# GpSimd takes the border sums of the second network, the border's roots follow directly, and a stage splits its first weight unit alone

## The reference

```python
for layer in range(DEPTH):
    u = rms_norm_2(h, norm_g[layer, 0]) * (1.0 + sc1) + sh1
    y = hgrn2_mixer(...) if layer % N_MIXERS == 0 else dilated_attention_mixer(...)
    h = h + (1.0 + g1) * rms_norm_2(y, norm_g[layer, 1])
    u = rms_norm_2(h, norm_g[layer, 2]) * (1.0 + sc2) + sh2
    y = swiglu_ffn(u, ffn_w_in[layer], ffn_w_out[layer])
    h = h + (1.0 + g2) * rms_norm_2(y, norm_g[layer, 3])
```

## Time and profile before

| | us |
|---|---|
| median of 3 runs (lowest to highest) | 3851.92 (3847.77 to 3854.98) |
| the profiled execution | 3851.2 |
| its span, first to last instruction | 3849.4 |
| PE busy | 3546.0 (92%) |
| DVE busy | 1979.5 (51%) |
| ACT busy | 1365.0 (35%) |
| POOL busy | 4.6 (0%) |

### The profile page before, as it was taken

One profiled execution on the slowest core, in us unless ns is written; L12 is line 12 of the kernel. 1 busy time (PEld: TensorE's weight loads), 2 busy tenths in 40 slices (PEclk: granted clock), 3 DMA queues, 4 the chain that ended last, 5 costly groups with the idle time before them and its releaser, 6 DMA issues.

```text
span 3849.4 us, 43254 instructions
## 1 busy us (share of the span) xinstructions
PE 3546.0 (92%) x18038; PEld 2888.2 (75%) x18038; DVE 1979.5 (51%) x2741; ACT 1365.0 (35%) x1914; POOL 4.6 (0%) x13
## 2 busy tenths in 40 slices
PE   7899988999999999789997997999879999969997
PEld 3685547888888755588886776888778888768886
DVE  5436446777445454465545556433455545563335
ACT  3322343422323333353345445422443333362223
POOL 0000000000000000000000000000000000000000
PEclk9999998999999999999998998999989999989998
DMA  4331013445443230145532221222222323212221
GB/s 173 131 117 54 11 33 107 135 153 164 132 142 119 79 104 0 44 149 176 183 110 66 55 66 55 88 90 96 77 73 66 93 68 88 65 55 98 89 96 47
DMA packets 366626, 360.68 MB, mean 94 GB/s; under 512 B 65072, under 2 KB 312031, under 8 KB 365024
## 3 DMA queue, kind: packets, MB, share of 16 engines
q1 hardware_dynamic: 366211, 357.84, 30.1%
q10 hardware_dynamic: 220, 0.07, 0.0%
HBM read 350.02 MB, written 4.72 MB: 92 GB/s over the span
## 4 chain that ended last, share of the span: by engine, by line
PE 44%; DVE 6%; ACT 6%; issue 2%; DMA 0%; SPq 0%; DVEq 0%; ACTq 0%
PE ps L402 38%; ACT second_w_hi L472 1%; PE ps L2503 1%; DVE second_w_lo L530 1%; DVE r_st L2397 1%; DVE sums L463 1%; PE ps L2524 1%; ACT second_scr L668 1%; PE ps L2526 1%; PE ps L2276 1%; PE ps L2513 1%; DVE second_scr L852 0%; DVE x_res L854 0%; DVE second_scr L679 0%; DVE sq L460 0%
## 5 line engine op out<-in xcount | busy, mean ns | idle before, releaser
L402 PE MATMUL ps<-second_h_hi,second_w_hi 128*128 128x512 f32 (+1 forms) x2216 | 833.4, 376 | 117.4 <-DVE second_h_lo L880 59.0
L402 PE MATMUL ps<-second_h_lo,second_w_hi 128*128 128x512 f32 (+1 forms) x2216 | 813.8, 367 | 0.0
L402 PE MATMUL ps<-second_h_hi,second_w_lo 128*128 128x512 f32 (+1 forms) x2216 | 813.3, 367 | 0.0
L530 DVE TENSOR_TENSOR second_w_lo<-ring,second_w_hi 128x2048 fp32r<-128x2048 f32 (+2 forms) x176 | 373.2, 2121 | 505.6 <-ACT second_w_hi L472 505.6
L402 PEld LDWEIGHTS ps<-second_h_hi,second_w_hi 128*128 128x128 f32 x2216 | 432.9, 195 | 185.2 <-issue 72.6
L402 PEld LDWEIGHTS ps<-second_h_lo,second_w_hi 128*128 128x128 f32 x2216 | 432.9, 195 | 63.6 <-issue 1.7
L402 PEld LDWEIGHTS ps<-second_h_hi,second_w_lo 128*128 128x128 f32 x2216 | 431.0, 194 | 65.4
L472 ACT ACTIVATE second_w_hi<-ring 128x2048 fp32r<-128x2048 f32 (+2 forms) x176 | 311.4, 1770 | 348.7 <-PE ps L402 337.1
L402 PE MATMUL ps<-h_mix_hi,w_hi 128*128 128x512 f32 (+3 forms) x776 | 276.7, 357 | 27.8 <-DVE h_mix_lo L695 17.7
L402 PE MATMUL ps<-h_mix_lo,w_hi 128*128 128x512 f32 (+3 forms) x776 | 273.1, 352 | 0.0
L402 PE MATMUL ps<-h_mix_hi,w_lo 128*128 128x512 f32 (+3 forms) x776 | 272.5, 351 | 0.0
(11 more groups left out here) (402 smaller groups left out, 5726.6 us busy)
## 6 DMA issues: line engine op xcount, KB each, us to landing
ring<-in_w_mlp SPq DMA_DIRECT2D x64, 1024.0 KB, 5.3
side_w<-in_ada_w SPq DMA_DIRECT2D x96, 512.0 KB, 4.3
ring<-in_ffn_w_in SPq DMA_DIRECT2D x44, 1024.0 KB, 5.1
side_w<-in_w_mod SPq DMA_DIRECT2D x80, 512.0 KB, 3.8
ring<-in_attn_w_in SPq DMA_DIRECT2D x48, 512.0 KB, 5.2
ring<-in_hgrn_w_in SPq DMA_DIRECT2D x32, 512.0 KB, 4.8
ring<-in_ffn_w_out SPq DMA_DIRECT2D x16, 1024.0 KB, 4.9
ring<-in_w_in SPq DMA_DIRECT2D x14, 1024.0 KB, 5.4
```

The lines of the kernel that those rows point to most:

```text
L402: mm = pe.matmul(acc, lhsT, rhs, start=k == 0 and wp == ap, stop=k == j.kt - 1 and wp == 1)
L530: dve.tensor_tensor(unit.place(unit.slot[1]), unit.place(M.ring[:, u % RING, :]), unit.place(unit.slot[0]), ALU.subtract).then_inc(*S.w_lo ...
```

## The change

Five edits. (1) `add_sums` runs on GpSimd in a queue of its own instead of on DVE; `sums_now` and `pending` go. (2) For the sums of the last border (`sums_last`, gain 7) the square with the gain and the product are left out and only one part of three is added, since only the first root is used there. (3) `BorderThread`: ACT takes the second root directly behind the first, without the yield between; DVE's steps begin at(1) instead of at(2), and so each one job earlier; ACT's scale and high parts come at(2) and at(3) instead of both at(3). (4) At the start of a stage unit 0 alone is split, then the threads at -1 run, then the other units. (5) Behind a summed job of the second half (`slow`), DVE splits a freed unit's low part one job later. The new flag `by_pool` is set nowhere, so the first network's squares stay where they are.

```diff
     def square_sums(self, act, j):
...
         act.activation(dst[:, 0, :], y, ACT.Square)
-        act.activation(dst[:, 2, :], y, ACT.Square, scale=g)
+        if not j.sums_last:
+            act.activation(dst[:, 2, :], y, ACT.Square, scale=g)
         act.activation(y, y, ACT.Identity, scale=g, bias=0.0).then_inc(*S["sums_act"].one)
-    def add_sums(self, dve, j):
+    def add_sums(self, pool, j):
...
         if fresh:
-            dve.tensor_tensor(acc[:, 1, :], y, x, ALU.mult).then_inc(*S["sums_added"].one)
+            pool.tensor_tensor(acc[:, 1, :], y, x, ALU.mult).then_inc(*S["sums_added"].one)
             return
         dst = self.scratch(j)
-        dve.tensor_tensor(dst[:, 1, :], y, x, ALU.mult).then_inc(*S["sums_dve"].one)
-        dve.wait_ge(S["sums_dve"].sem, S["sums_dve"].at(S["sums_dve"].sent))
-        dve.wait_ge(S["sums_added"].sem, S["sums_added"].at(j.sum_nth))
-        dve.tensor_tensor(acc, acc, dst, ALU.add).then_inc(*S["sums_added"].one)
+        parts = slice(0, 1 if j.sums_last else 3)
+        if not j.sums_last:
+            pool.tensor_tensor(dst[:, 1, :], y, x, ALU.mult).then_inc(*S["sums_product"].one)
+            pool.wait_ge(S["sums_product"].sem, S["sums_product"].at(S["sums_product"].sent))
+        pool.wait_ge(S["sums_added"].sem, S["sums_added"].at(j.sum_nth))
+        pool.tensor_tensor(acc[:, parts, :], acc[:, parts, :], dst[:, parts, :], ALU.add).then_inc(*S["sums_added"].one)
+
+    def gpsimd(self, pool):
+        S, M = self.S, self.M
+        for j in self.jobs:
...
+            if j.sums:
+                self.add_sums(pool, j)
+        yield 0
     def scalar(self, act):
-        u = 0
+        u = 1
+        self.high(act, 0)
+        yield -1
         while u < len(self.units) and self.freed(u) < 0:
             self.high(act, u)
             u += 1
-        yield -1
     def vector(self, dve):
-        u, pending = 0, None
+        u = 1
+        self.low(dve, 0)
+        yield -1
         while u < len(self.units) and self.freed(u) < 0:
             self.low(dve, u)
             u += 1
-        yield -1
...
-            if pending:
-                self.add_sums(dve, pending)
-            pending = None
-            if j.sums and j.sums_now:
-                self.add_sums(dve, j)
-            elif j.sums:
-                pending = j
-            while u < len(self.units) and self.freed(u) <= j.at:
+            while u < len(self.units) and self.freed(u) <= j.at - j.slow:
                 self.low(dve, u)
                 u += 1
 class NormThread(Thread):
-    def high_parts(self, act, step):
+    def high_parts(self, act, step, pace=0.5):
         for i in range(self.n_batches):
-            yield self.at(step + i // 2)
+            yield self.at(step + int(i * pace))
 class BorderThread(NormThread):
     def scalar(self, act):
...
         act.preload_act_table_set("natural_log")
-        yield self.at(2)
         act.wait_ge(S["post_mean"].sem, S["post_mean"].at(n + 1))
...
-        yield from self.high_parts(act, 3)
+        yield from self.high_parts(act, 2, 1)
     def vector(self, dve):
-        yield self.at(2)
+        yield self.at(1)
...
-        yield self.at(3)
+        yield self.at(2)
         self.residual(dve, 1)
         self.product(dve, 1)
         for i in range(self.n_batches):
-            yield self.at(4 + i)
+            yield self.at(3 + i)
     def summed(js, gain):
-            j.sums_now = b == KD - 1
+            j.sums_last, j.slow = gain == 7, a > 0
```

More of the change, by code:

```diff
@@ L250, in __init__ @@
         self.needs, self.after, self.weights_first = needs, after, weights_first
-        self.square, self.wide, self.sums = square, None, None
+        self.square, self.wide, self.sums, self.by_pool, self.slow = square, None, None, False, False
 def cut(w, r0, r1, c0, n=UNIT, jobs=()):
@@ L453, in add_sums @@
         for sig, n in j.sums_after:
-            dve.wait_ge(sig.sem, sig.at(n))
-        dve.wait_ge(S["sums_act"].sem, S["sums_act"].at(j.sum_nth + 1))
+            pool.wait_ge(sig.sem, sig.at(n))
+        pool.wait_ge(S["sums_act"].sem, S["sums_act"].at(j.sum_nth + 1))
         if fresh:
-            dve.tensor_tensor(acc[:, 1, :], y, x, ALU.mult).then_inc(*S["sums_added"].one)
+            pool.tensor_tensor(acc[:, 1, :], y, x, ALU.mult).then_inc(*S["sums_added"].one)
             return
         dst = self.scratch(j)
-        dve.tensor_tensor(dst[:, 1, :], y, x, ALU.mult).then_inc(*S["sums_dve"].one)
-        dve.wait_ge(S["sums_dve"].sem, S["sums_dve"].at(S["sums_dve"].sent))
-        dve.wait_ge(S["sums_added"].sem, S["sums_added"].at(j.sum_nth))
-        dve.tensor_tensor(acc, acc, dst, ALU.add).then_inc(*S["sums_added"].one)
+        parts = slice(0, 1 if j.sums_last else 3)
[7 more added lines that the diff above has]
+        for j in self.jobs:
+            if j.by_pool:
+                n = j.n
+                for done, added, nth, dst, i in ((S.sq_act, S.sq_add, j.square_nth, j.square[1], 0),
+                                                 (S["wide_act"], S["wide_add"], j.wide_nth, j.wide[1], 1)):
+                    pool.wait_ge(done.sem, done.at(nth + 1))
+                    pool.wait_ge(added.sem, added.at(nth))
+                    pool.tensor_tensor(dst, dst, M.sq[:, i, 0:n], ALU.add).then_inc(*added.one)
+            if j.sums:
+                self.add_sums(pool, j)
+        yield 0
     def high(self, act, u):
@@ L552, in vector @@
                                   ALU.subtract).then_inc(*S.lo.one)
-            if j.square:
+            if j.square and not j.by_pool:
                 _, dst, fresh = j.square
@@ L559, in vector @@
                     dve.tensor_tensor(dst, dst, M.sq[:, 0, 0:n], ALU.add).then_inc(*S.sq_add.one)
-            if j.wide:
+            if j.wide and not j.by_pool:
                 _, dst, fresh, _ = j.wide
@@ L600, in _ @@
                 weave(self.vector(dve), [s.vector(dve) for s in self.sides])
+            @block.gpsimd
+            def _(pool):
+                weave(self.gpsimd(pool), [s.gpsimd(pool) for s in self.sides])
 class NormThread(Thread):
```

## The result

The changed kernel takes 3813.14 us (median of 4 runs, 3810.15 to 3815.70) against 3849.9 us for the kernel before (4 runs, 3847.77 to 3854.98): a ratio of 0.9902, 95% interval 0.9885 to 0.9919. The forecast was 3816. The profiled execution took 3815.24 us, its span is 3813.4 us, 36.0 less than before; the forecast's sum was 35.5. The mean granted clock hardly moved (0.964 against 0.961).

What follows compares the result with a forecast made beforehand. PE was busy 92% of the span, so only its idle gaps could give time. Starts 12.5, borders 11, 4, 12 and 5, less 9 for collisions, make 35.5 off 3851.5: 3816 us, range 3794 to 3838.

Steps and rivals of the forecast that it cites:

- Starts, 12.5: Starts of the three planned stages: PE begins sooner as unit 0 is split alone first; 12.5 us saved.
- A half job on GpSimd, 2.6 us: Border sums: product 0.63, add 1.88 and handover 0.1 on GpSimd make 2.6 us a half job, against DVE's 1.4.
- 4.3 later: First border, first half: GpSimd's slower chain ends the sums at 2372.2 instead of 2367.9, 4.3 us later.
- Rival B: Border sums: GpSimd runs near DVE's rate, 1.2 us less per half job, 22 less in all, 3794; chance 0.13.
- From the sums to the low part, 16.8: First border: path from the sums to the first low part of the activations takes 16.8 us instead of 32.4.
- The sizes of the borders without collisions: Gains before collisions: first border 11 us, second 4, third 12, last 5.
- Last border, 5: Last border: one part of three and no product, so the sum stops holding PE and the tail shortens; 5 us saved.
- `slow` and `by_pool` I cost at nothing: Second half: `slow` puts a low part behind an evacuation it would await anyway; `by_pool` is set nowhere; 0 us.
- rival D: Starts gain as said, but borders only trade waits except the last one's 5 us: 3834; chance 0.17.
- Collisions, 9: Borders: DVE and GpSimd meet in one low part and two later adds; 3 us lost at each of three, 9.
- rival A: Full lock: two-input DVE operations and all GpSimd operations exclude each other; 9 us more, 3825; chance 0.20.
- C: GpSimd paces the borders, each extra us of a half job costing 33 us; about 3864 at 5.2 us; chance 0.08.

Runs made afterwards that it cites:

- runs 4 and 2: First: changed kernel with the border's root and step order and the stage starts as before, 3854.0 us; second: only the border's order as before, 3841.68 us.
- run 6: Changed kernel in which GpSimd fills its scratch with a constant in place of product and addition, same signals, output not the reference's: 3799.53 us.
- run 12: Changed kernel (sums on GpSimd) with DVE's low part of a freed unit no longer one job later in the second half: 3835.22 us.
- run 7: Changed kernel with GpSimd's product and additions cut to two columns each, the rest not added up: 3785.08 us.
- run 3: Changed kernel with its sums back on DVE in their earlier places, all other edits kept: 3793.99 us.
- run 5: Changed kernel with sums back on DVE, while GpSimd runs additions of the same length on unused memory that nobody waits for: 3842.13 us.

## Why the prediction was right

**Starts, 12.5.** Right. The first matmul of the third stage was forecast at 1588.4 and came at 1586.36, with 2.03 us brought from ahead of the stage. The idle at the three starts fell by 1.80, 2.20 and 9.39 us, against 1.9 (0.9 of it kept), 2.2 and 9.4 forecast. The whole term measured 12.3, 12.3 alone (14.6 by the medians), 11.9 between runs 4 and 2.

**A half job on GpSimd, 2.6 us.** Right: 1.80 for the addition, 0.73 for the product and 0.08 between them. "4.3 later" for the first border's sums: 3.5 in run 6 (2356.50 with that kernel's 15.0 of earlier time, against the 2367.97 at which the matmul started before), 7.4 in the changed kernel, where the collision behind the second job adds the rest. Rival B (GpSimd at DVE's rate) fell with it. The Trainium skill ("GPSIMD Engine Reference", section "Performance versus the Vector engine") had led to an estimate of 2.4 us; the trace has 2.6, near to it and far from DVE's 1.4.

**From the sums to the low part, 16.8.** Right without collisions (17.2, run 6), 19.4 in the changed kernel (2363.00 to 2382.42), where a unit's low part that collides (3.60 us at 2377.01) ends 1.8 us after the activations' high part that the next instruction needs (2378.79). The sizes of the borders without collisions were forecast at 11, 4, 12 and 5, and run 6 has 12.5, 5.4, 15.6 and 7.4: 40.9 instead of 32.

**Last border, 5.** Measured 6.9, and the wait for the first half's sum is gone as forecast. The kernels without edit 3 (6.8, 7.6) and those with the sums on DVE (6.8 to 7.9) have it too. What all of them share is edit 2 (only one of three sums in the last border), so it looks like the cause; no run has it alone.

**"`slow` and `by_pool` I cost at nothing"** is the step that failed, in its half on `slow`. I read edit 5 as moving a low part behind an evacuation in the second half's own border. But the summed jobs of the second half are the ones that run while the first half's border is worked on. Edit 5 therefore puts DVE's low part of a unit behind the border's next steps instead of ahead of them: in the changed kernel it stands behind the residual of the second four blocks (2377.01, the residual at 2372.59), in run 12 ahead of it (2373.38, the residual at 2376.43). ACT's high part of the unit stays where it was. My path of 16.8 has no low part of a unit on DVE, so it holds only with edit 5; the sum was right, but it credited edit 3 with what edits 3 and 5 earn together. Without edit 5 the three borders gain nothing (+5.8, run 12) and the kernel takes 3835.22 us, near rival D's 3834 (the borders only trade waits), though the wait that does it, the second batch's 7.68 us, is none of those that D named.

**Collisions, 9.** Mis-sized. Run 6 differs from the changed kernel by 17.2 us over all borders; its half job is 0.17 us shorter, worth 1.5 by run 7's 8.8 us for each us, so some 15 are the collisions (12 by the medians: 13.6 less 1.8). I had one low part and two meetings a border; the profile shows four low parts of 3.60 us and more at the first alone, and one of them at the worst place, ahead of an evacuation. The lock of rival A is real: the trace has 5.24 us for a 2.29 us operation that met one of 3.42, and run 6, in which GpSimd reads nothing, has no low part above 2.30 us. The Trainium skill ("SBUF — State Buffer", section "SBUF: two separate sides") says that the lock is exclusive, and the trace agrees. A's price of 18 in all was nearer to this than my 9. Its time (3825) was wrong, and mine right, because the 8 us that the borders lost beyond my 9 (17.2) and the 9 us that they gained beyond my 32 (40.9) cancel. That is luck: the total is better than its parts.

**The move as a whole** I had as a price of 11.6 (4.3, 4.8 and 2.5) and 9, with no name for what DVE gains by it. By the runs the 17.0 are: a chain slower by 0.95 us a half job (2.61 against 1.66), at 8.8 some 8.4; collisions, about 15; and 6 to 7 back, which I take to be DVE's relief. By the medians the same working on 19.2 gives 10, 12 and 3 back. These three are worked out, not each measured alone: that the collisions are the largest holds either way, but how much is given back, and by what, stays open.

**C** (GpSimd as the pace of the borders) held 33 us for each us of a half job; measured, it is 8.8 to 10.8 between 1.10 and 2.44 us. I take it that PE's own half jobs hide the rest, which no run shows. No run has half jobs longer than 2.6 us, so C's turning point of 3.9 us stays untested.

**D** also named matmuls that run slower for a while after a stop. The trace has them: a matmul of 256 columns takes 0.28 us ahead of the stop of 6.42 us and 0.41 behind it, and over the three borders PE is busy 1208.0 us in the changed kernel, 1202.3 before. My sum has no term for these 5.7 us. A slip of its last lines: the chances of the forecast, A, B and D add up to 0.92, not 0.91.

**What would show it:** idle of the third start under 7 (5.74), the addition near 1.9 (1.80 to 1.97), 819 waiting about 6 (5.08), the gap near 2 (2.46), the new stall about 5 (6.93), the last border's wait gone: all there. (819 is the number that line 803 has now.) Not foreseen: the 6.42 us at 2346.08.

The version that beats both kernels and still computes the reference is run 3, 3793.99 us: all of the change but its first edit.

## What to carry to other kernels

Before work is moved from VectorE to GpSimd, list VectorE's two-input operations that will run beside it, and add up to the whole of the other's duration to each that meets one on the path. Here an engine with half its time free was still the better place.

An edit that only changes which of two ready instructions goes first in a queue can be worth as much as the large ones (here 22 us). Look up which jobs run while the critical chain is worked on, and ask which foreign instruction the edit takes out from between the chain's steps.

When a forecast's total is right, test its terms anyway: two of mine were off by 6 to 9 us in opposite directions, and one carried 22 without a name. And compare medians as well as profiled executions: one profile can be its kernel's fastest or slowest run, which here moved a difference of 17 us by 3.

## What the runs showed of the hardware

DVE's two-input operations and GpSimd's additions hold each other up: 2.29 us became 5.24, 3.60 and 3.85 in the changed kernel, DVE's 768-element addition 0.96 became 1.63 in the mean (run 5), and GpSimd's product 0.72 became up to 2.78. In all DVE was busy 22.8 us longer for the same instructions (1929.5 against 1906.7 in run 6). DVE's evacuation from PSUM was not held up: it took 0.41 us in the middle of a GpSimd addition (2376.67, above). GpSimd's fills, which read nothing, left DVE's low parts at 2.291 us in the mean (run 6). GpSimd's two-input price where nothing collides is 0.72 us for 256 elements, 1.80 for 768 and 3.42 for 1536, and 0.20 us remain at two columns (run 7).
